# A 31-tap causal convolution split between TensorE and VectorE: two feature tiles as diagonal matmuls become four as packed column tiles

## What is computed

```python
def _conformer_conv(a, gate, conv_w, conv_b, ln_g, ln_b, w_out):
    u = a * jax.nn.sigmoid(gate)
    u = lax.conv_general_dilated(
        u, conv_w[:, None, :].astype(u.dtype), window_strides=(1,),
        padding=[(CONV_WIDTH_2 - 1, 0)], dimension_numbers=('NWC', 'WIO', 'NWC'),
        feature_group_count=CONV_CH) + conv_b
    u = jax.nn.silu(_layernorm(u, ln_g, ln_b))
    return u @ w_out
```

## Time and profile before

| | |
|---|---|
| median of three runs | 960.56 us |
| the profiled execution, its own time | 960.79 us |
| its span in the trace | 958.7 us |
| TensorE busy | 947.3 us, 99% |
| VectorE busy | 691.0 us, 72% |
| ScalarE busy | 540.0 us, 56% |
| DMA | 164.6 MB, mean 172 GB/s |
| granted clock of TensorE | 0.999 of full speed |

### The profile page before, as it was taken

One profiled execution on the slowest core, in us unless ns is written; L12 is line 12 of the kernel. 1 busy time (PEld: TensorE's weight loads), 2 busy tenths in 40 slices (PEclk: granted clock), 3 DMA queues, 4 the chain that ended last, 5 costly groups with the idle time before them and its releaser, 6 DMA issues.

```text
span 958.7 us, 14407 instructions
## 1 busy us (share of the span) xinstructions
PE 947.3 (99%) x5487; PEld 820.6 (86%) x5487; DVE 691.0 (72%) x1198; ACT 540.0 (56%) x952; POOL 15.2 (2%) x20
## 2 busy tenths in 40 slices
PE   9999999999999999999999999999999999999997
PEld 7999987788888888889999998888878888888885
DVE  5658985377776666666589998897786676666665
ACT  6645677745655445555354557664755665445453
POOL 0300000000000000000000000000000000000000
PEclk9999999999999999999999999999999999999999
DMA  8754444655465555555654354444465346655551
GB/s 315 223 177 136 139 144 132 198 185 184 159 219 183 192 191 183 176 176 185 188 171 140 125 166 153 131 129 162 138 219 182 103 156 227 210 196 180 176 176 44
DMA packets 87091, 164.60 MB, mean 172 GB/s; under 512 B 7344, under 2 KB 9712, under 8 KB 86896
## 3 DMA queue, kind: packets, MB, share of 16 engines
q1 hardware_dynamic: 86656, 163.56, 52.5%
q10 hardware_dynamic: 368, 0.14, 0.1%
HBM read 162.56 MB, written 1.05 MB: 171 GB/s over the span
## 4 chain that ended last, share of the span: by engine, by line
PE 95%; ACT 2%; DVE 1%; issue 1%; POOLq 0%; POOL 0%; ACTq 0%; DVEq 0%
PE pb L380 92%; PE pb L384 3%; ACT whi L895 1%; ACT YC L1212 0%; DVE LNS L1822 0%; ACT ZT L895 0%; ACT GA L1035 0%; ACT L1212 0%; ACT L1035 0%; DVE GA L1691 0%; ACT S L1350 0%; DVE XS L2028 0%; DVE wlo L1402 0%; ACT GC L1035 0%; DVE OT L1461 0%
## 5 line engine op out<-in xcount | busy, mean ns | idle before, releaser
L1402 DVE TENSOR_TENSOR wlo<-raw,whi 128x1024 fp32r<-128x1024 f32 (+2 forms) x300 | 356.7, 1212 | 144.7 <-ACT whi L895 143.9
L895 ACT ACTIVATE whi<-raw 128x1024 fp32r<-128x1024 f32 (+2 forms) x302 | 310.2, 1047 | 158.1 <-PE pb L380 154.9
L380 PE MATMUL pb<-XT,whi 128*128 128x256 f32 (+1 forms) x1552 | 375.0, 324 | 1.5 <-issue 1.5
L380 PE MATMUL pb<-XT,wlo 128*128 128x256 f32 (+1 forms) x1032 | 290.7, 282 | 0.0
L380 PEld LDWEIGHTS pb<-XT,whi 128*128 128x128 f32 x1552 | 258.6, 190 | 29.3 <-issue 3.8
L380 PE MATMUL pb<-whi,ZT 128*128 128x512 f32 x640 | 202.0, 392 | 0.4 <-DVE wlo L1402 0.4
L380 PEld LDWEIGHTS pb<-XT,wlo 128*128 128x128 f32 (+1 forms) x1032 | 195.9, 190 | 0.5
L380 PE MATMUL pb<-whi,XT 128*128 128x512 f32 x448 | 153.3, 406 | 0.0
L380 PEld LDWEIGHTS pb<-whi,ZT 128*128 128x128 f32 x640 | 120.2, 188 | 27.0 <-DVE wlo L1402 1.7
L380 PE MATMUL pb<-wlo,ZT 128*128 128x512 f32 x320 | 124.7, 390 | 0.0
L380 PEld LDWEIGHTS pb<-whi,XT 128*128 128x128 f32 x448 | 84.2, 188 | 18.6 <-issue 1.3
(11 more groups left out here) (208 smaller groups left out, 755.4 us busy)
## 6 DMA issues: line engine op xcount, KB each, us to landing
raw<-in_w_in SPq DMA_DIRECT2D x107, 512.0 KB, 3.5
raw<-in_w_ff SPq DMA_DIRECT2D x64, 512.0 KB, 4.5
raw<-in_w_up SPq DMA_DIRECT2D x32, 512.0 KB, 4.4
raw<-in_w_down SPq DMA_DIRECT2D x32, 512.0 KB, 4.7
raw<-in_w_branch_b SPq DMA_DIRECT2D x8, 512.0 KB, 4.5
raw<-in_w_out SPq DMA_DIRECT2D x8, 512.0 KB, 5.6
raw<-in_wx_kv SPq DMA_DIRECT2D x8, 512.0 KB, 4.4
raw<-in_w_attn_out SPq DMA_DIRECT2D x8, 512.0 KB, 3.2
```

What stands on the lines that cost most here:

```text
L380: return e.matmul(o, l, r, start=start, stop=stop, skip_group_check=True)
L895: return e.activation(o, i, ACT.Copy, scale=scale)
L1402: e.tensor_tensor(wlo[u % NW][:, 0:c], raw[u % NRAW][:, 0:c], whi[u % NW][:, 0:c].bitcast(F32), ALU.subtract).then_inc(lo, 1)
```

## The change

`PE_CONV` becomes 4: VectorE keeps tiles 0 to 3 (124 operations), TensorE takes tiles 4 to 7. The diagonals, `conv_out` and their semaphores go. In their place:

- 32 channels and four taps fill the 128 partitions. `U4[32*j + c, f, g, n]` holds channel 32*g + c of tile 4+f, shifted by j columns. It lies on `ZT` and the first columns of `OT`, which become one tensor `ZO`. SyncE fills it by 16 SBUF to SBUF DMAs of 32 partitions x 4 x 283 or 284 columns, four ahead of each of four loads (those of `b2_k1`'s last unit and the first three of `b2_q0`). The first four wait for `conv_in(1)` and for a small memset.
- `WQ[n]`, 128 x 8 x 4 x 32 for each tile, holds for eight groups q of four taps a block of four 32x32 diagonals, one for each tap, stacked on the partitions. VectorE makes each of the four with one `tensor_tensor` of 1024 columns, with two broadcast inputs, right after `conv_in(0)`.
- After the 14th, 16th, 18th and 20th unit from `b2_cg1` on, TensorE does one whole tile: 8 q x 4 g matmuls with 128 rows, 32 columns and 256 moving columns, each g in its own 32 columns of the array and its own 32 partitions of bank 6 or 7. ScalarE adds the bias on the way out (`conv_outs`).

The host adds 128 columns to the parameters and 32 to the constants, and `DG` shrinks from 512 to 260 columns. The diff, its core:

```diff
-PE_CONV = 6
+PE_CONV = 4
...
-        DG = sb("DG", 4 * P)
+        DG = sb("DG", 260)
...
+        U4 = ZO[:, 0:4544].bitcast(F32).rearrange("p (f g n) -> p f g n", g=4, n=284)
+        WQ = [work(W0 + a, f"WQ{i}", 1024)[:, :].rearrange("p (q g c) -> p q g c", q=8, g=4)
+              for i, a in enumerate((0, 1024, 16240, 17264))]
...
+                if u == b2 + 28:
+                    e.wait_ge(*out_at["b2_ca1", 3])
+                    e.wait_ge(u4_zero, 1)
+                if b2 + 28 <= u < b2 + 32:
+                    j = u - b2 - 28
+                    a = 1 if j == 0 else 0
+                    for g in range(4):
+                        e.dma_start(U4[32 * j:32 * j + 32, :, g, a:284],
+                                    U2[32 * g:32 * g + 32, 4:8, j + a - 1:j + 283]).then_inc(u4_in, 16)
...
             def conv_taps():
-                for _ in range(10):
-                    yield
-                for f in range(PE_CONV, 8):
-                    e.wait_ge(*out_at[f"b2_ca{f // 4}", f % 4])
-                    for k in range(31):
-                        n = 31 * (f - PE_CONV) + k
-                        e.wait_ge(dg_made, n + 1)
-                        mm(PB[f][:, 0:256], DG[:, P * (n % 4):P * (n % 4) + P], U2[:, f, k:k + 256], k == 0,
-                           k == 30).then_inc(cv_done, 1)
-                        if n % 2:
-                            yield
+                for _ in range(13):
+                    yield
+                e.wait_ge(u4_in, 256)
+                for n in range(4):
+                    e.wait_ge(wq_made, n + 1)
+                    if n >= 2:
+                        e.wait_ge(cv_out, n - 1)
+                    for q in range(8):
+                        for g in range(4):
+                            i = mm(PB[6 + n % 2][32 * g:32 * g + 32, 0:256], WQ[n][:, q, g, :],
+                                   U4[:, n, g, 4 * q:4 * q + 256], q == 0, q == 7)
+                    i.then_inc(cv_done, 1)
+                    yield
+                    yield
...
-            def diagonals():
...
+            def conv_outs():
+                for _ in range(14):
+                    yield
+                for n in range(4):
+                    e.wait_ge(cv_done, n + 1)
+                    e.activation(YC[:, 4 + n, :], PB[6 + n % 2][:, 0:256], ACT.Identity,
+                                 bias=prm("convb2", 4 + n)).then_inc(cv_out, 1)
+                    yield
+                    yield
...
             conv_in(0)
+            e.memset(U4[0:32, :, :, 0:1], 0.0).then_inc(u4_zero, 1)
+            for n in range(4):
+                e.tensor_tensor(WQ[n].rearrange("p q g c -> p (q g) c"),
+                                CST[:, CS["eye4"]:CS["eye4"] + 32].unsqueeze(1).broadcast_to([P, 32, 32]),
+                                prm("convq", 32 * n, 32).unsqueeze(2).broadcast_to([P, 32, 32]),
+                                ALU.mult).then_inc(wq_made, 1)
             taps = taps2()
...
+            e.wait_ge(cv_done, 4)
...
-            conv_out(7)
```

More of the change, by code:

```diff
@@ L25 @@
                   ("lng", 8), ("lnb", 8), ("normx", 8), ("normmem", 8), ("normffn", 8), ("qg", 1), ("kg", 3),
-                  ("posk", 16), ("posv", 16)):
+                  ("posk", 16), ("posv", 16), ("convq", 128)):
     PRM[_name] = _n
@@ L29 @@
 NPRM = _n
-CS = {"ident": 0, "ones": 128, "dist": 256, "causal": 640, "mhalf": 1024, "end": 1025}
+CS = {"ident": 0, "ones": 128, "dist": 256, "causal": 640, "mhalf": 1024, "eye4": 1025, "end": 1057}
 C2 = {"cbias": 0, "cmask": 480, "end": 960}
@@ L57, in build @@
         XT = sb("XT", 8 * 512, F32R)
-        ZT = sb("ZT", 8 * 512, F32R)
-        OT = sb("OT", 8 * 512, F32R)
+        ZO = sb("ZO", 16 * 512, F32R)
+        ZT, OT = ZO[:, 0:8 * 512], ZO[:, 8 * 512:16 * 512]
         X = sb("X", 2 * D)
@@ L307, in build @@
         wi_t, wi_out, ki_moved = sem("wi_turned"), sem("wi_copied"), sem("ki_moved")
-        dg_made, cv_done, y_made, cv_out = sem("diagonal_made"), sem("conv_tap_done"), sem("y_made"), sem("conv_copied")
+        wq_made, u4_zero, cv_done, y_made, cv_out = (sem(x) for x in (
+            "conv_blocks_made", "u4_zeroed", "conv_tile_done", "y_made", "conv_copied"))
+        u4_in = sem("u4_landed")
         ln_tiles, ln_sum, ln_mu, ln_sub, ln_sq, ln_sqs, ln_var, ln_sd, ln_norm, silu_done = (sem(x) for x in (
@@ L741, in attention2 @@
                         e.wait_ge(*out_at[f"b2_v{h // 4}", 1])
-                        e.wait_ge(*(o_lo, 4 + h) if h else (cv_out, 1))
+                        e.wait_ge(*(o_lo, 4 + h) if h else (cv_out, 3))
                         o = PB[6]
@@ L1310, in scalar_program @@
             e.dma_start(KI[64:128, :], KW[0:64, :]).then_inc(ki_moved, 16)
-            side, diag = attention2(), diagonals()
+            side, outs = attention2(), conv_outs()
             for name in ("b2_cg1", "b2_ca1", "b2_k0", "b2_k1", "b2_q0", "b2_q1"):
-                run(name, side, diag)
+                run(name, side, outs)
                 if name == "b2_cg1":
@@ L1316, in scalar_program @@
                 elif name != "b2_ca1":
+                    if name == "b2_q0":
+                        e.wait_ge(cv_done, 2)
                     copy_cols(name, KT2 if name[3] == "k" else QT2, 4 * int(name[4]))
             for name in ("b2_v0", "b2_v1", "b2_gc0", "b2_gc1"):
-                run(name, side, diag)
+                run(name, side, outs)
                 if name[3] == "v":
@@ L1323, in scalar_program @@
                         copy_out(name, t, V2[:, t, 512 * i:512 * i + 512])
-            run("b2_ga0", side, diag)
-            now(diag)
+            run("b2_ga0", side)
             norm = conv_norm()
@@ L1783, in attention2 @@
                         factors((s - 27) // 2, 16)
-                    if s == 27:
-                        conv_out(6)
                     h = (s - 30) // 2
@@ L1812, in taps2 @@
                                 yield
-            def conv_out(f):
-                e.wait_ge(cv_done, 31 * (f - PE_CONV) + 31)
-                e.tensor_scalar(YC[:, f, :], PB[f][:, 0:256], prm("convb2", f), None, ALU.add).then_inc(cv_out, 1)
             def conv_norm():
@@ L2093, in constants @@
     c[:, CS["mhalf"]] = -0.5
+    c[np.arange(P), CS["eye4"] + np.arange(P) % 32] = 1.0
     q, k = np.arange(P)[:, None], np.arange(2 * P)[None, :]
@@ L2128 @@
         params[:, PRM[name]:PRM[name] + v.shape[1]] = v
+    w = np.zeros((32, D), np.float32)
+    w[1:] = I["conv_w_2"].reshape(31, D)
+    params[:, PRM["convq"]:] = w.reshape(8, 4, 8, 4, 32)[:, :, 4:].transpose(1, 4, 2, 0, 3).reshape(P, 128)
     for r in (0, 64):
```

## The result

The changed kernel takes 952.26 us, the median of four runs (952.18 to 953.24). The kernel before, on the same chip, takes 960.47 us (four runs, 959.76 to 960.90). The ratio is 0.9920, with a 95% interval from 0.9908 to 0.9931. The prediction was 950.7 us in a range from 949.2 to 955.5: the direction and most of the size held, and the time came out 1.6 us above the forecast. The profiled execution of the changed kernel took 952.18 us.

What follows compares the result with a forecast made beforehand. The prediction took TensorE, busy for 99% of the span, as the bound. It summed 960.79 - 26.7 + 15.3 + 1.75 - 0.1 - 0.35 = 950.7 us, with a range from 949.2 to 955.5.

Steps and rivals of the forecast that it cites:

- The removed pairs and the packed tiles, -26.7 and +15.3: On TensorE: 31 pairs of taps removed at 0.86 us each, four packed feature tiles added at 3.8 us each.
- strict order: Rival at the packed tiles: passes start strictly in program order, 7.25 us a feature tile, 964.4 us in all; 8%.
- VectorE's lag at `b2_k0`, +1.75: At the start of `b2_k0`: VectorE's four new operations delay the products emptying the banks, so TensorE's stall grows 1.75 us.
- The copies into `U4`, "in 3.6 us early": Before the first packed tile: 16 SyncE copies land by 531.8, TensorE asks at 535.4, so no wait.
- a cover fails: Rival at `b2_k0` or first packed tile: VectorE's four operations take longer or copies land late, 953 to 955 us; 8%.
- Layer norm, -0.35: At the layer norm's start: TensorE's wait for VectorE's reduction shrinks 0.35 us, as VectorE no longer does `conv_out(7)`.
- Start, -0.1: At the kernel's start: 80 KB more parameters and constants, but a smaller memset lets TensorE start sooner; together -0.1 us.
- "The 62 operations ... are worth nothing": In the rows stretch: removing VectorE's operations for tiles 4 and 5 gains nothing, since TensorE is the later one there.

## Why the prediction was right, and where not

- *The removed pairs and the packed tiles, -26.7 and +15.3.* Right. The passes start in fours, each four within 40 ns, four tiles share the array with no loss, and a tile costs 3.8 us. The Trainium skill's page TensorE: Matmul & The Clock Gate, Part 3, has a gain of 2.38 for three column tiles. The trace shows more for four: 64 passes in 3.66 us, a gain of 13.8 / 3.66 = 3.8. (By that figure of the Trainium skill the prediction's sum would be 3.6 us worse, 17.4 - 13.8, not 3.7.) The same part of the Trainium skill's page has matmuls start and end strictly in order. The traces disagree, if the two passes of a matmul are neighbours: strict order gives 7.25 us a tile by the prediction's working, and 3.8 were measured. With one column set in a row it would let only one pass overlap at each change of set, 61 x 0.216 = 13.2 us, and 11.50 were measured.
- *VectorE's lag at `b2_k0`, +1.75.* Right in place, cause and nearly in size: the wait grew from 1.01 to 2.48 us, by 1.47. The four operations took 1.22 us each and were not dearer for their two broadcasts.
- *What follows from that wait: missing.* The prediction counted the idle time and nothing behind it. The granted clock was at the lower level from 518.0 to 521.4, and the first unit of `b2_k0` took 1.5 us more. The kernel before with only the four operations shows it alone: a wait longer by 1.9 us cost 3.5.
- *The copies into `U4`, "in 3.6 us early": wrong.* They started 0.9 us sooner than foretold and were late all the same. The issue was taken from the load of the earlier trace rows at 0.47 us and measured 0.61, so the last of sixteen was issued at 530.4 instead of 527.8. The landing was taken as 3.6 to 4.0 us, and the middle one measured 5.3 and the longest 6.7. So all were in by about 537.1 instead of 531.8. The first four, issued while the DMA engines' share was 0.48, landed in 2.7 us, and the other twelve, with a share of 1.05 (0.42 before the change), in 5.7. That full engines made them slow fits this, but was not tested by itself. TensorE waited 1.02 us, +1.1 from start to start. The landing of a lone load, read in a stretch with half-idle engines, was the wrong row for sixteen copies that share the engines with weights. The prediction held this for a rival of 8% (a cover fails) and priced it as part of up to 4.6 us; it is that rival that came, in a small size, beside the forecast.
- *Layer norm, -0.35.* Right. From the matmul before to the one that needs the reduction, 0.64 us (662.56 to 663.20) became 0.27 (654.41 to 654.68), and the wait is gone.
- *Start, -0.1.* The traces can't tell. The first matmul starts at 1.19 instead of 1.45, and `b2_cg0` begins 0.65 us sooner. But the first weight product is already 0.88 us sooner (10.39 instead of 11.27), and in the traces of the experiments on the changed kernel, whose start is the same, it begins anywhere from 9.46 to 11.04.
- *"The 62 operations ... are worth nothing": nearly, but not shown from the rows.* With VectorE's old load TensorE waits 0.8 us in the heads' steps, 1.2 from start to start. The prediction looked at one place, the first head, where the slack was 0.15 us. The waits came at the sixth and seventh of eight heads (transposes at 633.9 and 641.0), after five without one.
- *The sum.* From `b2_cg0` to the end: -26.7 + 15.2 + 1.5 (wait) + 1.5 (clock) + 1.1 (copies) - 0.4 (layer norm) = -7.8, where the two traces differ by 8.4 - 0.65 = 7.7. The prediction has -10.0 for the same stretch. The two missing terms, 1.5 and 1.1, less 0.3 for the lag, are those 2.3 us. The profiled execution came out only 1.5 us above the forecast, since it was 0.65 us ahead at `b2_cg0`, where 0.1 was foretold, and since its time exceeds its span by 0.2 us less than before the change. How much of that is the change and how much the single execution, the traces don't show. So part of how near the forecast lies is luck.

## What to carry to other kernels

When TensorE is the bound, price an added wait with what comes after it: here waits of 2.5 and 2.9 us at `b2_k0` cost another 1.5 by the clock, while one of 1.0 cost nothing beyond itself. Two late things in one stretch hide each other, and removing one only shows the other; remove them together before judging any (1.1 us at most for one, 5.6 for all). And a stand-in for removed work must copy its dependences as well as its count, or it measures its own chain.

## What the runs showed of the hardware

- Idle time of TensorE and the granted clock behind it: waits of 1.0 us (the kernel before, that with two operations, and the first packed tile of the changed kernel) left it at 1.00. Behind waits of 2.48 and 2.94 us at `b2_k0` it was 0.51 from 518.0 to 521.4, behind one of 2.03 at the packed tile 0.59 from 535.1 to 538.5, and behind one of 3.29 it was 0.50 and 0.53 from 535.1 to 541.9.
- Float32 matmuls in four column sets, 32 columns each, overlap fully when neighbours in the program differ in their columns (3.66 us for 64 passes), and hardly at all when they don't (11.50 us): then only four passes of a set run beside four of the next, at each change of set.
- A copy of 142 KB between parts of SBUF, from 32 partitions to 32 others, took 0.61 us of SyncE's queue in the median. The first four landed in 2.7 us. The other twelve took 5.7 beside the stream of weights, while the DMA engines' share was 1.05.
- A tap operation on VectorE (128x256) starts some 0.52 us after the one before when it waits for it, and 0.40 us after it in two chains: four take 1.94 and 1.58 us until the next operation.
